# A hybrid mixer with 64 experts: sixteen slabs of the input projection as seven block products, with weight sums by accumulating transfers

## What is computed

```python
h = rms_norm(x, norm_mix[l])
proj = h @ w_in[l]
u_s5, x_lru, g_lru, p_rw, z_ssd, xbc_ssd, dt_ssd = _split(
    proj, [S5_W, LRU_W, LRU_W, RW_COLS, SSD_W, SSD_XBC, SSD_HEADS])
y_s5 = s5_mixer(u_s5, ...)
y_lru = rglru_mixer(x_lru, g_lru, ...)
y_rw = rwkv7_mixer(p_rw, ...)
y_ssd = ssd_mixer(z_ssd, xbc_ssd, dt_ssd, ...)
x = x + (jnp.concatenate([y_s5, y_lru, y_rw, y_ssd], axis=-1) @ w_out[l]).astype(x.dtype)
h = rms_norm(x, norm_ffn[l])
x = x + hier_moe(h, ...)
```

## Time and profile before

| | |
|---|---|
| median of three executions | 2472.53 us |
| the profiled execution, its time and its span | 2467.88 us, 2465.9 us |
| granted clock of TensorE, mean | 0.979 |
| TensorE busy | 2275.0 us |
| VectorE busy | 870.9 us |
| GpSimd busy | 513.8 us |
| ScalarE busy | 376.5 us |
| projection, from the first L2583 to the last L2618 | 23 to 597 us |

### The profile page before, as it was taken

One profiled execution on the slowest core, in us unless ns is written; L12 is line 12 of the kernel. 1 busy time (PEld: TensorE's weight loads), 2 busy tenths in 40 slices (PEclk: granted clock), 3 DMA queues, 4 the chain that ended last, 5 costly groups with the idle time before them and its releaser, 6 DMA issues.

```text
span 2465.9 us, 32922 instructions
## 1 busy us (share of the span) xinstructions
PE 2275.0 (92%) x12955; PEld 1226.1 (50%) x12955; DVE 870.9 (35%) x1319; ACT 376.5 (15%) x658; POOL 513.8 (21%) x636
## 2 busy tenths in 40 slices
PE   8999999999999999899988888888888988888888
PEld 4444448886566646544444444444444444444443
DVE  5799876557544332411111111111111111111114
ACT  3000152215222222000000000000000000000002
POOL 3566316541322110111111101101111111110110
PEclk9999999999999999999999999999999999999999
DMA  6222213323202345999999999999999999999998
GB/s 190 69 68 68 74 52 94 86 70 101 97 26 79 112 162 202 368 421 427 425 425 426 426 425 426 427 425 426 427 426 426 427 426 424 427 426 425 425 426 361
DMA packets 151301, 717.78 MB, mean 291 GB/s; under 512 B 34264, under 2 KB 89884, under 8 KB 107452
## 3 DMA queue, kind: packets, MB, share of 16 engines
q1 hardware_dynamic: 123416, 693.51, 69.0%
q0 software_dynamic: 18432, 16.83, 2.0%
q10 hardware_dynamic: 9380, 6.40, 0.8%
HBM read 719.68 MB, written 47.19 MB: 311 GB/s over the span
## 4 chain that ended last, share of the span: by engine, by line
PE 48%; DMA 42%; DVE 7%; issue 1%; POOL 0%; ACT 0%; DVEq 0%; POOLq 0%; ACTq 0%
DMA big<-in_moe_w 42%; PE ps L2956 11%; PE ps L2618 8%; PE ps L2678 6%; PE ps L2583 6%; DVE big L1514 3%; PE ps L2987 3%; PE ps L2833 2%; PE ps L2753 1%; PE ps L2972 1%; PE ps L2738 1%; DVE big L1646 1%; DVE big L1645 1%; PE ps L2997 1%; PE ps L2632 1%
## 5 line engine op out<-in xcount | busy, mean ns | idle before, releaser
L2956 PE MATMUL ps<-big 128*64 128x384 f32 x4096 | 696.3, 495 | 105.4 <-DMA big<-in_moe_w 94.1
L2956 PEld LDWEIGHTS ps<-big 128*64 128x64 f32 x4096 | 308.9, 138 | 499.6 <-issue 318.4
L2987 PE MATMUL ps<-big 128*64 128x512 f32 x1536 | 376.9, 643 | 56.9 <-DVE big L2313 56.9
L2583 PE MATMUL ps<-big 128*128 128x512 f32 (+1 forms) x672 | 293.2, 594 | 0.0
L2309 DVE TENSOR_SCALAR big<-ps,scal 128x384 f32<-128x384 f32 x64 | 39.6, 619 | 702.4 <-PE ps L2956 698.3
L2987 PEld LDWEIGHTS ps<-big 128*64 128x64 f32 x1536 | 122.7, 147 | 264.0 <-issue 233.0
L2318 DVE SCALAR_TENSOR_TENSOR big<-ps,scal,big 128x512 f32<-128x512 f32 x128 | 90.2, 747 | 389.3 <-PE ps L2987 389.3
L2583 PEld LDWEIGHTS ps<-big 128*128 128x128 f32 (+1 forms) x672 | 125.6, 189 | 163.8 <-issue 163.7
L1039 POOL COPY scal<-slots 128x3 f32 (+1 forms) x64 | 11.8, 186 | 900.7 <-DVE big L2318 886.0
L2618 PE MATMUL ps<-big 128*128 128x256 f32 x896 | 196.4, 379 | 0.0
L2618 PEld LDWEIGHTS ps<-big 128*128 128x128 f32 x896 | 169.5, 190 | 24.8 <-issue 2.3
(11 more groups left out here) (435 smaller groups left out, 1982.1 us busy)
## 6 DMA issues: line engine op xcount, KB each, us to landing
big<-in_moe_w SPq DMA_DIRECT2D x187, 3072.0 KB, 39.0
big<-in_w_in SPq DMA_DIRECT2D x10, 2048.0 KB, 8.3
big<-in_w_in SPq DMA_DIRECT2D x32, 512.0 KB, 3.8
big<-in_moe_w SPq DMA_DIRECT2D x6, 1536.0 KB, 23.5
big<-in_w_out SPq DMA_DIRECT2D x8, 1024.0 KB, 5.4
big<-y_rows SPq DMA_DIRECT2D x8, 1024.0 KB, 27.5
big<-in_x SPq DMA_DIRECT2D x4, 1024.0 KB, 8.6
big<-in_x SPq DMA_DIRECT2D x16, 256.0 KB, 3.6
```

The lines of the kernel that those rows point to most:

```text
L2583: last = nc.tensor.matmul(ps[n % 2][0:wd, :], ring[s % 2][:, k, c:c + wd], hT[:, k, :], start=(k == 0), stop=(k == NC - 1))
L2956: last = nc.tensor.matmul(ps[2 + w][B * g:B * g + B, 0:FF], xT[k][:, j, B * g:B * g + B], W13[k][w][:, NJ * g + j, :], start=(j == 0), sto ...
L2987: last = nc.tensor.matmul(ps[5 + q][B * g:B * g + B, :], hid[k][:, m, :], W2[k][:, m, 512 * n:512 * n + 512], start=(m == 0), stop=(m == F ...
```

## The change

Sixteen slabs instead of eight go as block products: all but the two of S5 and the LoRA slab. The weights of a fast slab lie in eight rotating places of 512 KB (`slot`), one for each product, and SP loads product `g`'s part when product `g - 7` is done. Six parts are loaded plainly (`parts`: A11 and A21 twice, A12 and A22 once; the A12 at S4's place is not loaded). S1, S2 and S3 come from transfers that GpSimd issues with an add on top of what the place holds (`sum1`, `sum2`, `sum3`); S4 is one GpSimd instruction. Some sums have the other sign, which ScalarE undoes while it copies out. GpSimd makes T1, T2 and T4 by five instructions ahead of all S5 work. The tables are made from angles: GpSimd adds the coarse and the fine turn and takes off whole turns (`wrap`, three instructions), and ScalarE takes the absolute value and two sines (`table`). The S5 groups and the LRU and SSD steps are placed between the products.

```diff
-        slabs = [(C_S5 + SW * i, SW) for i in range(C_R // SW)] + [(C_XBC + SW * i, SW) for i in range((C_DT - C_XBC) // SW)] \
-            + [(C_LORA, LW + LA + LG)]
-
-
-        fast_slabs = [C_Z + SW * i for i in range(W // SW)] + [C_R + SW * i for i in range(3 * W // SW)]
+        slabs = [(C_S5 + SW * i, SW) for i in range(W // SW)] + [(C_LORA, LW + LA + LG)]
+
+
+        fast_slabs = [C_S5 + W + SW * i for i in range((C_R - C_S5 - W) // SW)] + [C_XBC + SW * i for i in range((C_DT - C_XBC) // SW)] \
...
+        SLOTS = 8
+        FIRST = 4 * (len(slabs) % 2)
+
+        def slot(f, b):
+            i = 16 + 2 * ((FIRST + PB_ * f + b) % SLOTS)
+            return big[:, i:i + 2, :].rearrange("p a n -> p (a n)").rearrange("p (c n) -> p c n", c=8)
+
+        def weights(f, name):
+            wv = I["w_in"][0].rearrange("(c p) n -> p c n", p=P)
+            i, k = int(name[1]) - 1, int(name[2]) - 1
...
-        products = [("A11", B11), ("A12", B21), ("S2", T2), ("S1", T1), ("S3", T3), ("S4", B22), ("A22", T4)]
+        sides = [B11, T1, T2, B22, T3, B21, T4]
+        parts = ["A11", "A21", "A11", "A12", "A21", "A12", "A22"]
+        B_S1, B_S2, B_S4, B_S3, B_A12 = 1, 2, 3, 4, 5
...
-                sp.wait_ge(sum_ok, SUMS + 4 * (f - 1) + 1)
-                load_quarter(f, "A21")
-                sp.wait_ge(sum_ok, SUMS + 4 * (f - 1) + 3)
-                sp.wait_ge(prod_ok, PROD + PB_ * (f - 1) + 1)
-                load_quarter(f, "A22")
...
+            for f in range(NF):
+                for b in range(PB_):
+                    g = PB_ * f + b
+                    if g == 0:
+                        sp.wait_ge(proj_ok, NT - 2)
+                    elif g == 4:
+                        sp.wait_ge(proj_ok, NT)
+                    elif f:
+                        sp.wait_ge(prod_ok, PROD + g - PB_ + 1)
+                    if b != B_S4:
+                        sp.dma_start(slot(f, b), weights(f, parts[b])).then_inc(weight_in[b], 16)
...
+            nc.gpsimd.tensor_tensor(T1, B11, B12, sub)
+            nc.gpsimd.tensor_tensor(T2, B12, B22, sub).then_inc(side_ok, 1)
+            pool.wait_ge(side_ok, SIDES + 1)
+            nc.gpsimd.tensor_tensor(T2, T2, B11, sub)
+            nc.gpsimd.tensor_tensor(T4, B22, T1, ALU.add).then_inc(side_ok, 1)
+            pool.wait_ge(side_ok, SIDES + 2)
+            nc.gpsimd.tensor_tensor(T4, T4, B21, sub).then_inc(side_ok, 1)
+
...
+            def wrap(p):
+                cosT, sinT = (s5tab[:, 2 * (p % 2) + r, :] for r in range(2))
+                if p >= 2:
+                    pool.wait_ge(tab_used, p - 1)
+                g.do(nc.gpsimd.tensor_tensor(cosT.rearrange("p (a b) -> p a b", a=COARSE),
+                                             turns[:, p, FINE:].unsqueeze(2).to_broadcast([P, COARSE, FINE]),
+                                             turns[:, p, 0:FINE].unsqueeze(1).to_broadcast([P, COARSE, FINE]), ALU.add))
+                g.settle()
+                g.do(nc.gpsimd.tensor_scalar(sinT, cosT, MAGIC, MAGIC, ALU.add, sub))
+                g.settle()
+                nc.gpsimd.tensor_tensor(sinT, cosT, sinT, sub).then_inc(wrap_ok, 1)
...
-                g.do(nc.gpsimd.tensor_tensor(t0, coarse[0], fine[0], ALU.mult))
-                g.do(nc.gpsimd.tensor_tensor(t1, coarse[1], fine[1], ALU.mult))
-                g.settle()
-                g.do(nc.gpsimd.tensor_tensor(cosT, t0, t1, ALU.subtract))
-                g.settle()
-                g.do(nc.gpsimd.tensor_tensor(t0, coarse[1], fine[0], ALU.mult))
-                g.do(nc.gpsimd.tensor_tensor(t1, coarse[0], fine[1], ALU.mult))
-                g.settle()
-                g.tell(nc.gpsimd.tensor_tensor(sinT, t0, t1, ALU.add), tab_ok, p + 1)
...
-            pool.wait_ge(conv_ok, WT)
-            sub = ALU.subtract
-            nc.gpsimd.tensor_tensor(T1, B12, B11, sub).then_inc(side_ok, 1)
-            pool.wait_ge(side_ok, SIDES + 1)
-            nc.gpsimd.tensor_tensor(T2, B22, T1, sub).then_inc(side_ok, 1)
-            pool.wait_ge(side_ok, SIDES + 2)
...
-                weight_sum(f, "S1", "A21", "A22", ALU.add)
+                weight_in_wait(f, B_S1)
+                nc.gpsimd.dma_start(slot(f, B_S1), weights(f, "A22"), accum_op=ALU.add).then_inc(s1_in, 16)
+
+            def sum2(f):
+                weight_in_wait(f, B_S2)
+                pool.wait_ge(s1_in, 16 * (f + 1))
+                nc.gpsimd.dma_start(slot(f, B_S2), slot(f, B_S1), accum_op=ALU.add).then_inc(s2_in, 16)
...
+                weight_in_wait(f, B_S3)
+                nc.gpsimd.dma_start(slot(f, B_S3), weights(f, "A11"), accum_op=ALU.add).then_inc(s3_in, 16)
...
+                weight_in_wait(f, B_A12)
+                pool.wait_ge(s2_in, 16 * (f + 1))
+                if f:
+                    pool.wait_ge(prod_ok, PROD + PB_ * f + B_S4 - SLOTS + 1)
+                nc.gpsimd.tensor_tensor(slot(f, B_S4), slot(f, B_A12), slot(f, B_S2), ALU.add).then_inc(s4_ok, 1)
...
+                    if b == 0 and f:
+                        sum4(f)
+                    if b == 3 and f < NF - 1:
+                        sum1(f + 1)
+                    if b == 4:
+                        add_held(f, 0)
...
+                        if f < NF - 1:
+                            sum2(f + 1)
...
+                    if b == 6:
+                        add_held(f, 2)
+                        if f < NF - 1:
+                            sum3(f + 1)
...
+                    p, off = divmod(PB_ * f + b + 12, 3)
+                    if off == 0 and p < NPAIR:
+                        wrap(p)
...
+            def table(p):
+                cosT, sinT = (s5tab[:, 2 * (p % 2) + r, :] for r in range(2))
+                act.wait_ge(wrap_ok, WRAP + p + 1)
+                a.do(nc.scalar.activation(cosT, sinT, ACT.Abs))
+                a.settle()
+                nc.scalar.activation(sinT, sinT, ACT.Sin, scale=6.283185)
+                nc.scalar.activation(cosT, cosT, ACT.Sin, scale=-6.283185, bias=halfpi[:]).then_inc(tab_ok, 1)
...
+            sc(S[12], ph(0)[:, :, 1], 0.25, None, ADD)
+            v.settle()
+            sc(S[13], S[12], MAGIC, MAGIC, ADD, SUB)
+            v.settle()
+            v.tell(nc.vector.tensor_tensor(S[12], S[12], S[13], SUB), setup_ok, PHASE2)
...
+            def s5_at(u):
+                step, off = divmod(u, S5_EVERY)
+                if off == 0:
+                    s5_step(step)
...
+                    if (n, k) == (2, 9):
+                        s5_inputs()
+                    if (n, k) == (2, 12):
...
-                    step, off = divmod(NC * (n - 3) + k - NC // 2, 13)
-                    if off == 0:
-                        s5_step(step)
+                    s5_at({3: -4, 5: 44}.get(n, -99) + 2 * k)
...
-                if n == 2:
-                    s5_inputs()
...
+                    s5_at(76 + 8 * g + k)
...
+                    if (f, b) == (6, 2):
+                        lru_gates()
+                    if (f, b) == (6, 3):
+                        s5_glu()
```

More of the change, by code:

```diff
@@ L483, in build @@
         took, TOOK = proj_got, NT
[L486 to L497 removed]
+        weight_in = [prm_in, prmB_in, s5_in, None, w_in_slot[0], w_in_slot[1], rs_ok]
+        WEIGHT_IN = [16 * len(PA), 16 * (len(PB) + 2), 16 * 8, 0, 16 * ((len(slabs) + 1) // 2), 16 * (len(slabs) // 2), NTT]
+        wrap_ok, WRAP = tr_used_act, 4
+        s1_in, s2_in, s3_in = xg_in[0], xg_in[1], y_out[0]
+        s4_ok, S4_OK = ldt_in, 16
+        FADD = 16 * NF
+        SLOTS = 8
[6 more added lines that the diff above has]
+            i, k = int(name[1]) - 1, int(name[2]) - 1
+            c0 = fast_slabs[f] + P * i
+            return wv[:, 8 * k:8 * k + 8, c0:c0 + P]
         TH = T // 2
@@ L1792, in rw_mix @@
                     x = (R_, K_)[step - 1]
-                    dve.wait_ge(added, ADDED + 3 * (W // SW) * (step + 1))
-                    dve.wait_ge(took, TOOK + PB_ * (W // SW) * (step + 1))
+                    slabs_done(dve, (R_END, K_END)[step - 1])
                     for k0 in (0, 2):
@@ L2596, in _ @@
                     s5_params()
-                if n == 2:
-                    s5_inputs()
-                if n == 18:
-                    s5_glu()
             def product(f, b):
-                name, side = products[b]
                 g = PB_ * f + b
@@ L2609, in product @@
                     pe.wait_ge(took, TOOK + g - 1)
-                if name[0] == "A":
-                    pe.wait_ge(a_in[name], A_IN[name] + 16 * (f + 1))
-                else:
-                    pe.wait_ge(sum_ok, SUMS + 4 * f + ({"S1": 1, "S3": 2, "S2": 3, "S4": 4} if f else {"S1": 1, "S2": 2, "S3": 3, "S4": 4})[name])
-                if f == 0 and b in (2, 4, 6):
-                    pe.wait_ge(side_ok, SIDES + {2: 2, 4: 4, 6: 4}[b])
-                w, o = quarter(f, name), bank_of(f, b)
+                if b == B_S1:
+                    pe.wait_ge(s1_in, 16 * (f + 1))
+                elif b == B_S2:
```

(13 more changed lines are left out.)

262 lines of the change are left out of this document (106 added, 156 removed).

## The result

The changed kernel took 2475.72 us (median of 17, 2471.31 to 2484.36) beside 2471.35 us (17 runs) of the kernel before: a ratio of 1.0024, interval 1.0017 to 1.0032, so 5.9 us slower by the ratio (the medians differ by 4.4, the spans of the two profiled executions, 2475.6 and 2465.9 us, by 9.7). The forecast was 2458. The change did what it says: the eight slabs are block products, nearly at the old pace, and the DMA share of the slabs rose from 0.21 and 0.32 to 0.85 and 1.08. (The share can pass 1, so it does not say by itself that the queues are full.) What it gained was spent again before 600 us.

What follows compares the result with a forecast made beforehand. TensorE, busy 92% of the span, was taken to bound the stage that changes. Terms of -27 + 13.9 + 2.5 + 0.9 = -9.7 us on the profiled 2467.9 gave 2458 us; own range 2450 to 2466, full range 2443 to 2500.

Steps and rivals of the forecast that it cites:

- rival 2: In the scan, a pair takes 13.5 to 14.5 us and TensorE waits 12 to 24 us: 2470 to 2482; chance 0.10.
- The block products: In eight slabs, seven products of 3.46 us replace a plain slab, gaining 3.4 us each: -27 us.
- The wait for Gin: Early TensorE transposes wait for GpSimd's copies, delayed by its five sums and two wraps: 13.9 us, inputs ready at 73.5.
- The convolutions: Before the LRU gates, TensorE has 11.7 us of work against 12.4, and a weight sum falls among them: 2.5 us.
- The scan: VectorE's pair takes 11.9 us against 12.3 that TensorE gives it, so TensorE waits 0 us.
- The clock: Expert matmuls run slower in some rounds after TensorE has waited: 0 to 1.7 us, taken as 0.9.
- Rival 1: At the start, the early sums hide, leaving a wait of 2.7 us and no clock loss: 2444; chance 0.20.
- Rival 3: In the slabs, accumulating transfers set the pace from 4.1 us apiece: 2503 at 5 us, 2545 at 5.9; chance 0.20.

Runs made afterwards that it cites:

- e3_both: Changed kernel with the five early sums on VectorE, S5 groups every 26 units instead of 24, and LRU gates and following steps four products later; 0.9964 of the kernel before.
- e1_ve_sums: Changed kernel with the five early sums of activations moved from GpSimd's start to VectorE's pause; 0.9979 of the kernel before.
- e8_wrap_cut: Changed kernel with the tables cut to 32 columns from the fifth pair on, so not made (measuring only); 0.9977 of the kernel before.
- e7: Changed kernel with S4 cut to each chunk's first column from the second slab on, so not summed (measuring only); 0.9963 of the kernel before.
- e5_later: e3_both with each table on ScalarE one product later; 0.9965 of the kernel before.
- e10_wrap_later: e9_setup_first with each wrap and its table one product later; 0.9916 of the kernel before.
- e6_best: e5_later with GpSimd's copies into Gin ahead of the first two wraps, and LRU gates and following steps another product later; 0.9969 of the kernel before.
- e9_setup_first: e6_best with ScalarE's first two tables behind its copies of Gin and C instead of ahead of them; 0.9919 of the kernel before.
- e11_s4_dma: Changed kernel with S4 also made by transfers: A12 loaded once more, then an accumulating transfer from S2's place; 1.0020 of the kernel before.

## Why the prediction was wrong

The range held the time; the sign was wrong. The forecast was -27 + 13.9 + 2.5 + 0.9 = -9.7, and the changed kernel came out 5.9 slower, inside my rival 2 (2470 to 2482, "the scan falls behind"), to which I gave 0.10. Of its mechanism half is seen: a pair took the 13.5 us that it names, but TensorE's waits in the scan were 6.1 us and not 12 to 24; the slow clock and ScalarE's copies made up the rest. Step by step:

- *The block products, -27.* Right in kind, 2 us too large: about 25 us, and 24.6 in the changed kernel's own profile (596.67 - 22.98 - 0.3 less 603.12 - 22.88 - 31.4). A product stays at 3.46 us where four follow each other (437.54 to 451.36), but three between two S5 groups take 10.56 us, 3.52 each (199.06 to 209.62). In e3_both, which has the least slow time, all block products take 391.2 us from start to start, and 194.0 in the kernel before: a new slab takes 24.65 where I took 24.2, and the plain ones that went had taken 27.73. That too makes 24.6.
- *The wait for Gin, 13.9.* Right: 13.2 us, at 72.78 where 73.5 was forecast. VectorE's dependent instructions pass only between GpSimd's sums, as forecast (VectorE's timeline of the changed kernel, where such an instruction alone takes 0.17 us, then GpSimd's), and e1_ve_sums shows that the early sums are the cause:

```profile
38.81 4.49 DVE L1535 TENSOR_TENSOR s5v<-colC,s5v 128x16 f32<-128x16 f32 x1
...
43.42 4.38 DVE L1539 TENSOR_SCALAR s5v<-s5v 128x16 f32<-128x16 f32 x1
```

```profile
38.75 4.52 POOL L854 TENSOR_TENSOR big<-big 128x2048 f32<-128x2048 f32 x1
43.23 4.54 POOL L855 TENSOR_TENSOR big<-big 128x2048 f32<-128x2048 f32 x1
...
68.35 4.37 POOL L882 COPY big<-big 64x64 f32<-64x64 f32 x16
```

- *The convolutions, 2.5.* Not called for here, by luck: 0.2 us at the gates, and 0.7 at a root mean square behind them. The weight sum that I had put among the convolutions had ended at 301.24, before they began at 301.69, since the scan was late. In e8_wrap_cut it falls among them (a sum at 287.60; the convolution at 286.56 takes 4.29 us for 2.32), and TensorE waits 2.35 us at the gates.
- **The scan, 0 us: the step that failed.** I took 11.9 us for a pair against 12.3 that TensorE gives it. Both were off. TensorE's pace is six products, one group of inputs and half a group of outputs for two pairs: 20.7 + 1.9 + 1.0 us, or 11.8 a pair, and 11.9 measured (in e8_wrap_cut, which has no wait in the scan, the inputs at 154.58 and those four pairs later at 202.29). I had divided over a stretch that held the lag of the last outputs too, 39 products where twelve pairs have 36, and had divided wrongly: 152 us for twelve pairs is 12.7. (So is the 12 us that I gave for a pair of 13.49: by my 12.3 it would be 14, by 12.7 it would be 10.) And a pair took 13.49, since I counted the wraps at 0 to 1.5 and took next to nothing of it: they cost 1.66, and the weight sum alone 1.14 where I took 1.4 for it and the held adds (e7, e8). So TensorE stood 6.1 us at the scan (3.6 at its inputs, 2.5 at its last outputs), where I had put nothing.
- **The clock, 0.9 us: mis-sized.** I looked at the experts alone. In the projection slow time was 8.0 us, behind waits as short as 1.53; 1.9 of it stands behind the wait for Gin (63 to 83 us), the other 6.1 behind waits of the scan (183, 233 and 293 us).
- *GpSimd's and ScalarE's order, not in the sum.* 3.2 us of waits for copies, at 138.74 and 279.49. I had named what is queued behind GpSimd's wait for Gin, and not what is queued behind its wraps. In both places ScalarE's table waits for a wrap, and the copy of a product stands behind the table:

```profile
136.51 0.63 ACT L1161 ACTIVATE big<-big 128x512 f32<-128x512 f32 x1 [8.53 <-POOL big L869]
```

  At 277.26 it is 5.26 us, and there GpSimd had itself stood 3.99 us at its issue of S2, for S1's transfer to land: the accumulating transfers cost no wait that names them, but they hold up GpSimd's program. With the tables later, held adds behind the wraps are what is left (e5_later), and with the wraps later too, nothing (e10_wrap_later).

With these the sum is -24.6 + 23.4 + 8.0 - 0.3 = 6.5, the 6.45 by which the projection ends later, beside the measured 5.9. That it closes proves little where the -24.6 is the remainder of the same profile; e3_both's products give it a second time. The expert matmuls begin 8.9 us later (1011.5 for 1002.6) and end 8.3 later, so their stage keeps its length, as forecast; where the 2.4 us between the projection and the experts come from was not traced.

Rival 1 (the early sums hide) fell with the 13.2 us. Rival 3 (accumulating transfers pace the slabs) did not come, though its price did: 3.9 us on average where I took 4, and 1.7 for a plain one where I took 2.0. The Trainium skill's reason (Collectives: The Full Stack, the bandwidth ceiling: a reduction at half a copy's rate) fits 3.9 beside 1.7 on average only: from SBUF an accumulating transfer costs 2.6, 1.5 times a plain one, and from DRAM about 4.5, 2.6 times. An issue on GpSimd takes 1.58 us (from DRAM, 136.43) and 0.92 (from SBUF, 145.53), nothing near 8.4; landing takes 6.9 and 5.3 us, not the estimate of 3.2, and still no product of the changed kernel waits for it. What was wrong in rival 3 is its point. I compared 24 us of transfers with 24.2 us of bare products. But S5, LRU and SSD matmuls stand between them: in the scan a slab has 7/6 of 23.6 us, 27.5. So the DMA share was 0.81, where I had 0.95 for a price of 4. At 22 us a slab no wait of the changed kernel names a transfer (e3_both, e5_later, e6_best and e9_setup_first have one each, of 0.6 to 1.0 us), at 26 (e11_s4_dma) five do, three of them in the scan; the point lies between or near these, and was not measured more closely.

Of the versions that compute the whole layer six beat both kernels, and e9_setup_first and e10_wrap_later most, with no difference between them that the runs show. e9_setup_first has the sums on VectorE, groups every 26 units, and Gin ahead of the tables on both engines; it is 20 us faster than before (0.9919). It keeps the gain of the block products and has 8.6 us of idle and slow time left of 31.4.

## What to carry to other kernels

When a change moves work ahead of a chain that a full engine waits for, look for an idle stretch of another engine first: the same five sums cost 11 us more on GpSimd's start than in VectorE's pause. On an in-order engine, list what stands behind each new wait two engines further, and move the work on all of them, or the wait may only change its name. Where two engines share a pace, work out both paces from the order of the instructions over one full period, and price every instruction that shuts the slower one out; a shortfall of 1.6 us in 12 appears as a few short waits, and the clock can add twice the length of each (3.3 us for the 1.53 here).
